# Splitting the gather of the next pair's tokens in a two-layer encoder's mixture of experts

## The chip, the cores and the metric

The kernel runs on one core of one Trainium2 chip. The metric is device time in microseconds (us) from start to end of one execution; the number given for a kernel is the median of its runs. TensorE (PE) does the matmuls, with its weight loads shown apart as PEld; VectorE (DVE) and ScalarE (ACT) read the matmul results out of PSUM; SyncE (SP) issues nearly all transfers from HBM.

## The reference

Two layers over 256 tokens of width 2048, all in float32. Each layer has three mixers (latent attention, dilated attention, an mLSTM), an output projection, and then the mixture of experts, in which alone this change lies:

```python
comb = jnp.sum(jax.nn.one_hot(eid, N_EXPERTS, dtype=f32) * w[..., None], axis=-2)
h = jax.nn.silu(jnp.einsum('bsd,edf->bsef', x, w_gate)) * jnp.einsum('bsd,edf->bsef', x, w_up)
h = h * comb[..., None].astype(h.dtype)
return jnp.einsum('bsef,efd->bsd', h, w_down)
```

There are 16 experts of width 512, and each token is routed to 2 of them. The gate, up and down weights of all 16 experts are 201 MB per layer (16 x 3 x 2048 x 512 x 4 bytes), and all of them are read from HBM in each layer.

## The kernel before

The five engines each have a program written out by hand, with semaphores between them. The experts are taken in 8 pairs per layer (`i` = 0 to 7). An expert has room for 64 tokens, so that a pair fills the 128 rows of the array: the two experts' matmuls stand alternately in TensorE's program, and each takes half of the columns.

For a pair, TensorE's program holds these blocks: the four products `g0`, `u0`, `g1`, `u1` (the first and second half of gate and up), `gather(i + 1)` (the next pair's tokens, picked out of `xtok` by a matrix of ones and zeros, `Gm`), `turn_h(0)` and `turn_h(1)` (transposes of the gated values), `scatter(i - 1)` in two halves, a transpose of the scatter weights, and the down products `dy0` to `dy3`. The gather writes four PSUM banks (`gx0` to `gx3`, banks 4 to 7, which the down products `dy0` to `dy3` use too), 8 matmuls of 128 columns into each. ScalarE copies these banks into `XG` only behind `u1` of the running pair, since the four products read `XG`. VectorE makes `Gm` in `tokens_of_pair`, with four small operations.

The expert weights come in blocks of 2 MB, 12 for each pair (two for each of `g0`, `u0`, `g1`, `u1`, `dn0`, `dn1`), in exactly that order, issued by SyncE. They land in nine slots, used in turn: six of `ring`, and the space of `BIAS`, `XN` and `PR`, which is why TensorE's rows show these names. A load waits until the block that was nine before it in the same slot has had its last reader. In each layer nine loads go out ahead of the experts; the tenth and eleventh then wait for the end of `g0` of pair 0, the next two for `u0`, the next two for `g1`, the next two for `u1`, and so on:

```python
EXPERT = [f"{n}{j}_{i}" for i in range(NE // 2) for n in ("g0", "u0", "g1", "u1", "dn0", "dn1") for j in range(2)]
EXPERT_SLOTS = (IN_BIAS, 5, 0, 1, 2, 3, 4, IN_XN, IN_PR)
```

All matmuls of the products, the gather, the scatter and the down products are recorded under one line (L642, the helper `mm`). They are told apart by their operands and shapes: the gather's read `v_mla` and `PR` (`Gm` lies in `v_mla`, the tokens in `PR`), those of the four products have the shape 128x256 at 64 weights' columns, the down products 128x512. One float32 matmul of the program is two records of the trace. `turn_h` is L986, the transpose of the scatter weights L1026. On VectorE, L1589 multiplies gate and up, and L1565 makes `Gm` and the scatter weights; SyncE's loads are L568.

Of the kernel before, what the change touches and what calls it, by code (L numbers as in the profile page):

```python
# [52 lines left out]
NE = NG * EPG  # L53
# [281 lines left out]
def build(nc, a, consts, onehot, lncount, out):  # L335
    with ExitStack() as ctx:
# [143 lines left out]
        def after(name, l, j=0, i=None, stride=0):  # L480

            s, n = stages[name]
            return s, l * n + (j + 1) + (0 if i is None else i * stride)
# [9 lines left out]
        def bank(name):  # L493
            return ps[:, BANKS.where(name), :]

        def ready(name, l=0):

            return psum_full[BANKS.where(name)], BANKS.before(name, l) + 1

        def freed(name, l=0):  # L500

            return psum_free[BANKS.where(name)], BANKS.before(name, l)

        def copied(name, l=0):

            return psum_free[BANKS.where(name)], BANKS.before(name, l) + 1

        def made(name):
            return psum_full[BANKS.where(name)], 1
# [4 lines left out]
        def slot(name):  # L514
            s = SLOTS.where(name)
            return ring[:, s, :] if s < NSLOT else spare[s]
# [15 lines left out]
        def loaded(name, l):  # L532
            s = SLOTS.where(name)
            return slot_full[s], 16 * (SLOTS.before(name, l) + 1)
# [105 lines left out]
        def _(pe):  # L640
            def mm(o, lhsT, rhs, start=True, stop=True):
                return pe.matmul(o, lhsT, rhs, start=start, stop=stop, skip_group_check=True)  # L642
# [154 lines left out]
            for l in range(DEPTH):  # L797
# [154 lines left out]
                mm(o[:, 2 * NE:3 * NE], ones[:, :], picked[:, 0, 0:NE], True, False)  # L952
                mm(o[:, 2 * NE:3 * NE], ones[:, :], picked[:, 1, 0:NE], False, True).then_inc(*made("rank"))

                def gather(i):

                    pe.wait_ge(*after("gm", l, i))
                    for n in range(4):
                        name = f"gx{n}_{i}"
                        pe.wait_ge(*freed(name, l))  # L960
                        for k in range(4):
                            d = (4 * n + k) * P
                            for t in range(NT):
                                last = mm(bank(name)[:, k * 2 * CAP:(k + 1) * 2 * CAP], xtok[:, t, d:d + P], Gm[:, t, :], t == 0, t == NT - 1)
                        last.then_inc(*made(name))

                def expert(n, i):

                    name = f"{n}_{i}"
                    w = [slot(f"{n}{j}_{i}").rearrange("p (k c) -> p k c", k=KT) for j in range(2)]  # L970
                    for j in range(2):
                        pe.wait_ge(*loaded(f"{n}{j}_{i}", l))
                    pe.wait_ge(*freed(name, l))
                    for k in range(KT):
                        for j in range(2):
                            own_rows = slice(j * CAP, (j + 1) * CAP)
                            last = mm(bank(name)[own_rows, 0:CH], XG[:, k, own_rows], w[j][:, k, :], k == 0, k == KT - 1)
                    last.then_inc(*made(name))

                def turn_h(half, i):  # L980

                    name = f"ht{half}_{i}"
                    pe.wait_ge(*copied(f"u{half}_{i}", l))
                    pe.wait_ge(*freed(name, l))
                    for q in range(2):
                        last = pe.transpose(bank(name)[:, q * 2 * CAP:(q + 1) * 2 * CAP], gated[:, (2 * half + q) * P:(2 * half + q + 1) * P], ident)  # L986
                    last.then_inc(*made(name))

                def scatter(i, ks):

                    for k in ks:
                        name = f"sc{k}_{i}"
                        pe.wait_ge(*freed(name, l))
                        for q in range(2):
                            last = mm(bank(name)[:, q * S:(q + 1) * S], Y[:, (2 * k + q) * P:(2 * k + q + 1) * P], Sw)
                        last.then_inc(*made(name))

                def written(i):
                    pe.wait_ge(*copied(f"sw_{i}", l))
                    for n in range(4):  # L1000
                        pe.wait_ge(*copied(f"dy{n}_{i}", l))
# [4 lines left out]
                for i in range(NE // 2):  # L1006
                    for n in range(4):
                        pe.wait_ge(*copied(f"gx{n}_{i}", l))
                    expert("g0", i)
                    expert("u0", i)  # L1010
                    expert("g1", i)
                    turn_h(0, i)
                    if i + 1 < NE // 2:
                        gather(i + 1)
                    expert("u1", i)
                    if i >= 1:
                        written(i - 1)
                        scatter(i - 1, range(KT // 4))
                    turn_h(1, i)
                    if i >= 1:  # L1020
                        scatter(i - 1, range(KT // 4, KT // 2))

                    pe.wait_ge(*freed(f"sw_{i}", l))
                    pe.wait_ge(*after("gw", l, i))
                    for t in range(NT):
                        last = pe.transpose(bank(f"sw_{i}")[0:2 * CAP, t * P:(t + 1) * P], Gw[:, t, :], ident)  # L1026
                    last.then_inc(*made(f"sw_{i}"))

                    for half in range(2):
                        pe.wait_ge(*copied(f"ht{half}_{i}", l))  # L1030
                    for half in range(2):
                        w = [slot(f"dn{half}{j}_{i}").rearrange("p (k c) -> p k c", k=4) for j in range(2)]
                        for j in range(2):
                            pe.wait_ge(*loaded(f"dn{half}{j}_{i}", l))
                        for q in range(2):
                            name = f"dy{2 * half + q}_{i}"
                            pe.wait_ge(*freed(name, l))
                            for k in range(4):
                                for j in range(2):
                                    own_rows = slice(j * CAP, (j + 1) * CAP)  # L1040
                                    last = mm(bank(name)[own_rows, :], hs[:, k, own_rows], w[j][:, k, q * 512:(q + 1) * 512], k == 0, k == 3)
                            last.then_inc(*made(name))
# [3 lines left out]
                with pe.If(due > 0):  # L1046

                    i = NE // 2 - 1
# [72 lines left out]
        def _(dve):  # L1121
# [121 lines left out]
            for l in range(DEPTH):  # L1243
# [324 lines left out]
                def tokens_of_pair(i):  # L1568
                    for j in range(2):
                        ins = one_hot(Gm[:, :, j * CAP:(j + 1) * CAP], 2 * i + j, seen)  # L1570
                    ins.then_inc(*signal("gm"))
# [10 lines left out]
                for n in (1, 3):  # L1582
                    gathered(f"gx{n}_0", n, l)
                for i in range(NE // 2):
                    for half in range(2):

                        dve.wait_ge(*copied(f"g{half}_{i}", l))
                        dve.wait_ge(*ready(f"u{half}_{i}", l))
                        dve.tensor_tensor(gated[:, half * CH:(half + 1) * CH], sgs[:, half * CH:(half + 1) * CH],  # L1589
                                          bank(f"u{half}_{i}")[0:2 * CAP, 0:CH], ALU.mult).then_inc(*read(f"u{half}_{i}"))  # L1590
                        if half == 0:
                            if i + 1 < NE // 2:
                                tokens_of_pair(i + 1)
                            for j in range(2):
                                ins = one_hot(Gw[:, :, j * CAP:(j + 1) * CAP], 2 * i + j, comb)
                            ins.then_inc(*signal("gw"))
                        elif i >= 1:
                            add_moe(i - 1, range(KT // 4))
                        dve.wait_ge(*ready(f"ht{half}_{i}", l))
                        dve.tensor_copy(hs[:, 2 * half:2 * half + 2, :].rearrange("p k n -> p (k n)"), bank(f"ht{half}_{i}")[:, 0:4 * CAP]).then_inc(*read(f"ht{half}_{i}"))  # L1600
                    if i >= 1:
                        add_moe(i - 1, range(KT // 4, KT // 2))
                    dve.wait_ge(*ready(f"sw_{i}", l))
                    dve.tensor_copy(Sw, bank(f"sw_{i}")[0:2 * CAP, 0:S]).then_inc(*read(f"sw_{i}"))
                    for n in (1, 3):
                        dve.wait_ge(*ready(f"dy{n}_{i}", l))
                        dve.tensor_copy(Y[:, n * 512:(n + 1) * 512], bank(f"dy{n}_{i}")[0:2 * CAP, :]).then_inc(*read(f"dy{n}_{i}"))  # L1607
# [356 lines left out]
```

## Time and profile before

| | |
|---|---|
| median of 3 runs | 1985.12 us (1984.39 to 1989.51) |
| the profiled execution | 1986.55 us, with a span of 1984.9 us |
| TensorE busy (matmuls) | 1929.6 us, 97% of the span |
| TensorE weight loads | 1457.5 us, 73% |
| VectorE, ScalarE, GpSimd busy | 472.4, 317.6 and 5.8 us |
| read from HBM | 534.49 MB, 270 GB/s over the span |
| mean granted TensorE clock | 0.989 of full speed |

The busy time of TensorE counts modelled ends of pipelined matmuls, so a busy share near 100% doesn't say that nothing waits: waits are read from the chain and from the start times. The expert stages of the two layers lie at about 538 to 990 us and 1521 to 1985 us. There the transfers are read for their rate (GB/s in a window), and each load for the time from its issue to its landing.

### The profile page before, as it was taken

What the parts mean: (1) busy time and instruction counts of PE and PEld (TensorE: products, weight loads), DVE (VectorE), ACT (ScalarE), POOL (GpSimd) and SP (SyncE); (2) the same over time, 40 slices, a digit from 0 to 9 for tenths busy, and PEclk for the clock granted to TensorE, in tenths of its full rate; (3) what the DMA queues carried; (4) which work ended last, traced back from release to release, by engine and by line L of the source; (5) the groups of instructions that cost most, each with busy time, mean ns of one, the idle gap of its engine ahead of it and who ended that gap; (6) DMA issues with size and microseconds to landing.
All of it is one profiled execution on the core that took longest, in us unless ns stands there. A gap on an engine that the chain in (4) does not pass through costs nothing.

```text
span 1984.9 us, 26562 instructions
## 1 busy us (share of the span) xinstructions
PE 1929.6 (97%) x11730; PEld 1457.5 (73%) x11730; DVE 472.4 (24%) x1233; ACT 317.6 (16%) x831; POOL 5.8 (0%) x12
## 2 busy tenths in 40 slices
PE   6999999999899999999899999999998999999998
PEld 6788888788766666656597888877887666666665
DVE  2233313122211111221133232222222012110212
ACT  2122122210211110111021221222102111110110
POOL 0000000000000000000000000000000000000000
PEclk9999999999899999999999999999998999999999
DMA  8353333223599999999963433322346999999995
GB/s 330 137 209 127 128 127 127 92 106 149 212 414 427 428 426 427 428 427 427 413 238 146 151 116 137 130 88 88 128 157 255 426 426 427 426 428 426 428 427 242
DMA packets 39831, 538.39 MB, mean 271 GB/s; under 512 B 4665, under 2 KB 4793, under 8 KB 7201
## 3 DMA queue, kind: packets, MB, share of 16 engines
q1 hardware_dynamic: 38160, 531.46, 65.3%
q0 software_dynamic: 1296, 5.13, 0.7%
q8 instruction: 97, 1.59, 0.3%
q14 instruction: 22, 0.17, 0.0%
q10 hardware_dynamic: 256, 0.04, 0.0%
HBM read 534.49 MB, written 2.12 MB: 270 GB/s over the span
## 4 chain that ended last, share of the span: by engine, by line
PE 97%; issue 1%; DVE 1%; DMA 1%; ACT 0%; SPq 0%; DVEq 0%
PE ps L642 94%; PE ps L693 1%; DMA ring<-in_w_lat 1%; PE ps L986 0%; PE ps L709 0%; PE ps L701 0%; PE ps L907 0%; PE ps L1026 0%; ACT PR L1849 0%; PE ps L780 0%; ACT L1862 0%; SPq L562 0%; DVE v_mla L1565 0%; PE ps L820 0%; DVE prob L1607 0%
## 5 line engine op out<-in xcount | busy, mean ns | idle before, releaser
L642 PE MATMUL ps<-ring,scr 128*64 128x256 f32 (+2 forms) x3520 | 562.7, 428 | 7.1 <-issue 7.1
L642 PE MATMUL ps<-ring,XN 128*128 128x256 f32 (+2 forms) x2304 | 484.6, 371 | 17.1 <-DMA ring<-in_w_lat 17.1
L642 PEld LDWEIGHTS ps<-ring,XN 128*128 128x128 f32 x2304 | 424.5, 191 | 66.9 <-issue 19.1
L642 PEld LDWEIGHTS ps<-ring,scr 128*64 128x64 f32 (+1 forms) x3520 | 319.8, 139 | 203.9 <-issue 113.2
L642 PE MATMUL ps<-XN,ring 128*128 128x256 f32 x768 | 170.4, 381 | 0.9 <-DVE prob L1155 0.9
L642 PE MATMUL ps<-BIAS,scr 128*64 128x256 f32 (+1 forms) x608 | 159.3, 420 | 6.9 <-issue 6.9
L642 PEld LDWEIGHTS ps<-XN,ring 128*128 128x128 f32 x768 | 144.7, 190 | 26.6 <-issue 7.7
L642 PE MATMUL ps<-PR,scr 128*64 128x256 f32 (+2 forms) x576 | 158.3, 430 | 0.7 <-DVE scr L1600 0.7
L642 PE MATMUL ps<-PR,ring 128*128 128x256 f32 x640 | 142.9, 383 | 0.0
L642 PE MATMUL ps<-XN,scr 128*64 128x256 f32 (+1 forms) x576 | 141.6, 403 | 0.3 <-issue 0.2
L642 PEld LDWEIGHTS ps<-PR,ring 128*128 128x128 f32 x640 | 121.9, 192 | 19.1 <-issue 2.7
L642 PE MATMUL ps<-v_mla,PR 128*128 128x128 f32 x1024 | 122.7, 283 | 4.1 <-DVE v_mla L1565 4.1
L642 PEld LDWEIGHTS ps<-v_mla,PR 128*128 128x128 f32 x1024 | 121.2, 200 | 4.2 <-issue 4.2
L642 PE MATMUL ps<-PR,prob 128*128 128x256 f32 x512 | 118.7, 386 | 5.0 <-issue 3.8
L1589 DVE TENSOR_TENSOR v_mla<-scr,ps 128x256 f32<-128x256 f32 x32 | 13.5, 421 | 429.8 <-PE ps L642 429.8
L642 PEld LDWEIGHTS ps<-PR,prob 128*128 128x128 f32 x512 | 96.0, 192 | 24.2 <-issue 12.1
L642 PEld LDWEIGHTS ps<-BIAS,scr 128*64 128x64 f32 x608 | 83.6, 139 | 34.2 <-issue 9.9
L642 PEld LDWEIGHTS ps<-PR,scr 128*64 128x64 f32 (+1 forms) x576 | 81.2, 146 | 34.6 <-issue 24.9
L642 PEld LDWEIGHTS ps<-XN,scr 128*64 128x64 f32 x576 | 78.3, 137 | 29.4 <-issue 19.5
L1874 ACT ACTIVATE scr<-ps,par 128x128 f32<-128x128 f32 x240 | 63.8, 412 | 222.7 <-PE ps L642 222.7
L1578 DVE TENSOR_TENSOR X<-X,ps 128x512 f32<-128x512 f32 x128 | 87.9, 687 | 31.9 <-PE ps L642 31.0
L1882 ACT ACTIVATE scr<-ps 128x256 f32<-128x256 f32 x32 | 12.3, 383 | 378.7 <-PE ps L642 378.7
(231 smaller groups left out, 1009.7 us busy)
## 6 DMA issues: line engine op xcount, KB each, us to landing
ring<-in_moe_w_up SPq DMA_DIRECT2D x44, 2048.0 KB, 22.7
ring<-in_moe_w_down SPq DMA_DIRECT2D x44, 2048.0 KB, 26.5
ring<-in_moe_w_gate SPq DMA_DIRECT2D x42, 2048.0 KB, 24.5
ring<-in_w_main SPq DMA_DIRECT2D x36, 2048.0 KB, 8.1
ring<-in_w_out_a SPq DMA_DIRECT2D x10, 2048.0 KB, 8.0
PR<-in_moe_w_down SPq DMA_DIRECT2D x10, 2048.0 KB, 24.2
XN<-in_moe_w_gate SPq DMA_DIRECT2D x10, 2048.0 KB, 28.2
BIAS<-in_moe_w_up SPq DMA_DIRECT2D x10, 2048.0 KB, 23.4
```

Source lines behind the costliest of these rows:

```text
L642: return pe.matmul(o, lhsT, rhs, start=start, stop=stop, skip_group_check=True)
L693: last = pe.transpose(bank(name)[:, (kt * NT + t) * P:(kt * NT + t + 1) * P], prob[:, u % 2, j, t, kt * P:(kt + 1) * P], ident)
L1578: dve.tensor_tensor(x, x, bank(name), ALU.add).then_inc(*read(name))
L1589: dve.tensor_tensor(gated[:, half * CH:(half + 1) * CH], sgs[:, half * CH:(half + 1) * CH], bank(f"u{half}_{i}")[0:2 * CAP, 0:CH], ALU.mul ...
L1874: ins = act.activation(XG[:, 4 * n + k, :], bank(name)[:, k * 2 * CAP:(k + 1) * 2 * CAP], ACT.Copy, scale=pcol(l, R_FFN + 4 * n + k))
L1882: act.activation(sgs[:, half * CH:(half + 1) * CH], bank(f"g{half}_{i}")[0:2 * CAP, 0:CH], ACT.Silu).then_inc(*read(f"g{half}_{i}"))
```

## The change

The gather of the next pair is called in two halves, two of its four PSUM banks each. The first half stands behind `g0`, the second behind `u0`; before, the whole gather stood behind `turn_h(0)`, between `g1` and `u1`. So that `Gm` is there in time, VectorE makes it at the head of the pair, ahead of the multiplication of gate and up, and waits first until the four banks of this pair's own gather are complete (its matmuls are the last readers of the old `Gm`). The number of matmuls, copies and loads stays the same. The last pair of a layer gathers nothing and keeps its order.

```diff
-                def gather(i):
+                def gather(i, ns=range(4)):
 
                     pe.wait_ge(*after("gm", l, i))
-                    for n in range(4):
+                    for n in ns:
...
                     expert("g0", i)
+                    if i + 1 < NE // 2:
+                        gather(i + 1, (0, 1))
                     expert("u0", i)
+                    if i + 1 < NE // 2:
+                        gather(i + 1, (2, 3))
                     expert("g1", i)
                     turn_h(0, i)
-                    if i + 1 < NE // 2:
-                        gather(i + 1)
                     expert("u1", i)
...
                 for i in range(NE // 2):
+                    if i + 1 < NE // 2:
+                        for n in range(4):
+                            dve.wait_ge(*ready(f"gx{n}_{i}", l))
+                        tokens_of_pair(i + 1)
                     for half in range(2):
...
                         if half == 0:
-                            if i + 1 < NE // 2:
-                                tokens_of_pair(i + 1)
                             for j in range(2):
```

On TensorE, in pair 0 of the first layer, the rows behind the last matmul of `g0` read as follows before (`u0` and `g1` are the matmuls on `ring`, the first of the 65 still belongs to `g0`; the row on `K,v_mla` is `turn_h(0)`, the row on `v_mla,PR` the gather, and the rows behind it begin `u1`):

```order
L642 MATMUL ps<-ring,scr 64x256 x65
L986 MATMUL ps<-K,v_mla 128x128 x2
L642 MATMUL ps<-v_mla,PR 128x128 x32
L642 MATMUL ps<-ring,scr 64x256
L642 MATMUL ps<-XN,scr 64x256
```

The same place on TensorE after the change:

```order
L642 MATMUL ps<-ring,scr 64x256
L642 MATMUL ps<-v_mla,PR 128x128 x16
L642 MATMUL ps<-ring,scr 64x256 x32
L642 MATMUL ps<-v_mla,PR 128x128 x16
L642 MATMUL ps<-ring,scr 64x256 x32
L986 MATMUL ps<-K,v_mla 128x128 x2
L642 MATMUL ps<-ring,scr 64x256
L642 MATMUL ps<-XN,scr 64x256
```

`u0` now stands behind 16 gather matmuls and `g1` behind 32, while `u1` follows `turn_h(0)` at once, behind the same number of matmuls as before.

On VectorE, the start of pair 0 before (L1589 is the multiplication of gate and up, L1565 makes `Gm` for the next pair and then the scatter weights, L1600 copies the turned values):

```order
L1589 TENSOR_TENSOR v_mla<-scr,ps 128x256 [waits psum_full1,psum_free0]
L1565 TENSOR_SCALAR v_mla<-PR 128x64 x8
L1600 COPY scr<-ps 128x256 [waits psum_full0]
L1589 TENSOR_TENSOR v_mla<-scr,ps 128x256 [waits psum_full3,psum_free2]
```

And after, where the same lines have the numbers L1595, L1567 and L1604:

```order
L1567 TENSOR_SCALAR v_mla<-PR 128x64 [waits psum_full6,psum_full7,psum_full5,psum_full4]
L1567 TENSOR_SCALAR v_mla<-PR 128x64 x3
L1595 TENSOR_TENSOR v_mla<-scr,ps 128x256 [waits psum_full1,psum_free0]
L1567 TENSOR_SCALAR v_mla<-PR 128x64 x4
L1604 COPY scr<-ps 128x256 [waits psum_full0]
```

Four of the eight small operations moved ahead of the multiplication, behind a wait for the four banks of the gather that has just been used.

## Rows read from the trace of the kernel before

**Rows 1.** The page: mean busy share of the DMA engines in 40 slices

```profile
DMA  8353333223599999999963433322346999999995
```

**Rows 2.** Windows: from:to, length, busy PE, PEld, DVE, ACT, POOL (count), PEclk, DMA share, GB/s

```profile
535.00:546.00 11.00, 9.95 (x93) 8.26 (x94) 0.69 (x1) 2.81 (x6) 0.00 (x0) 1.00 0.01 1
546.50:576.00 29.50, 28.47 (x256) 22.44 (x254) 3.81 (x13) 2.44 (x10) 0.00 (x0) 1.00 1.00 415
...
577.00:700.00 123.00, 123.00 (x892) 80.09 (x889) 21.90 (x47) 14.60 (x47) 0.00 (x0) 1.00 1.00 426
...
830.00:960.00 130.00, 123.86 (x916) 82.10 (x916) 22.94 (x52) 12.78 (x41) 0.00 (x0) 0.99 1.01 428
```

**Rows 3.** The chain in order of time, first layer: start, us, what

```profile
745.56 0.22 PE ps L1026 x2
...
802.28 0.22 PE ps L1026 x2
...
830.20 1.63 issue
...
888.77 1.98 issue
890.75 8.81 PE ps L642 x64
...
949.60 7.13 PE ps L642 x64
...
957.10 2.30 issue
959.40 12.46 PE ps L642 x80
```

**Rows 4.** The chain in order of time, second layer

```profile
1812.94 0.62 issue
...
1870.98 2.65 issue
...
1939.87 2.50 issue
```

**Rows 5.** Time to landing: loads issued at 545.5, 552.4, 559.3, 573.9 and 935.6

```profile
DMA to landing us min/median/max: 8.1/8.1/8.1
...
DMA to landing us min/median/max: 12.0/12.0/12.0
...
DMA to landing us min/median/max: 14.9/14.9/14.9
...
DMA to landing us min/median/max: 10.1/10.1/10.1
...
DMA to landing us min/median/max: 23.7/23.7/23.7
```

**Rows 6.** Timeline of SyncE: start, us, and the loads issued from then on

```profile
545.54 0.33 SPq L568 DMA_DIRECT2D BIAS<-in_moe_w_down  x1
545.91 6.86 SPq L568 DMA_DIRECT2D ring<-in_moe_w_down  x2
552.82 6.86 SPq L568 DMA_DIRECT2D ring<-in_moe_w_gate  x2
559.72 14.54 SPq L568 DMA_DIRECT2D ring<-in_moe_w_up  x2
```

**Rows 7.** Timeline of TensorE in pair 0: the gather of pair 1

```profile
559.52 7.31 PE L642 MATMUL ps<-v_mla,PR 128*128 128x128 f32 x64
```

**Rows 8.** Windows of 1 us, and of the last `g1` and `u1` of the layer (columns as in rows 2)

```profile
1559.00:1560.00 1.00, 1.00 (x6) 0.35 (x4) 0.00 (x0) 1.00 (x6) 0.00 (x0) 1.00 1.07 295
...
949.60:956.50 6.90, 6.90 (x64) 5.38 (x64) 1.21 (x5) 0.00 (x0) 0.00 (x0) 1.00 1.01 425
...
959.40:968.10 8.70, 8.70 (x64) 6.42 (x64) 0.00 (x0) 0.00 (x0) 0.00 (x0) 0.80 1.01 429
```

**Rows 9.** Timeline of VectorE in pair 2: copy of `dy3`, and the small operations

```profile
646.27 0.69 DVE L1607 COPY prob<-ps 128x512 f32<-128x512 f32 x1 [6.17 <-PE ps L642]
...
660.49 1.87 DVE L1565 TENSOR_SCALAR v_mla<-PR 128x64 f32<-128x64 f32 x8
```

## The prediction

> **What bounds the kernel now.** I read the page first: TensorE is 97% busy, and in the two expert stages the DMA engines are at 9 of 10 in every slice, where they are at 2 to 4 in most of the others [rows 1]. So two things may bound these stages, and the page can't say which. The windows say more of the transfers: nothing moves between 535 and 546 us, and from 546.5 us on the rate is 415, then 426, then 428 GB/s to the end of the layer's experts [rows 2]. From 546.5 us the DMA engines never stop, while TensorE still has spare time in the last 130 us (123.9 of 130 us busy).
>
> The chain in order of time says where TensorE waits. In the middle pairs it waits for nothing: the same row of two successive pairs stands 56.72 us apart (745.56, 802.28). Late in the layer three pieces "issue" appear, 1.63, 1.98 and 2.30 us, ahead of `g1` of pairs 5 and 6 and of `u1` of pair 7 [rows 3]. The second layer has the same places, with 0.62, 2.65 and 2.50 us [rows 4]. They are waits for weights. The load issued at 935.6 us lands 23.7 us later, at 959.3 us, and `u1` of pair 7 starts at 959.40 us [rows 3, 5]. Counted in order, that load is 76 places behind the one issued at 573.9 us, which landed 10.1 us later, at 584.0 us [rows 5]. So one load of 2 MB takes (959.3 - 584.0) / 76 = 4.94 us of the stream, and the 12 of a pair take 59.3 us. TensorE needs 56.7 us for a pair. It eats up the lead of the prefetch by 2.5 us a pair, and from pair 5 on it waits.
>
> Hence the last wait, `u1` of pair 7, is the one that sets the end of the layer. Its time is that of its load, which is the time at which the stream began to run without a pause, plus a fixed number of loads. The earlier waits don't add to it: TensorE, had it not waited before, would only wait longer there.
>
> **The change part by part.** *What moves on TensorE.* A gather takes 7.31 us [rows 7], half of it 3.66 us. `u0` ends 3.66 us later than before, `g1` 7.31 us later, `u1` at the same time. In pairs 5 and 6 this puts 7.3 us of work ahead of `g1`, where the waits of 1.63 and 1.98 us stand, so these vanish. Pair 7 has no gather, its order is unchanged, and the load that it waits for comes when the stream delivers it. By the argument above the vanished waits reappear in pair 7. The gain from them is 0.
>
> *What it does to the stream.* Here is the price. In pair 0 the stream is fed by the slots that `g0`, `u0`, `g1` and `u1` let go: two loads at 545.5 us, two at 552.4, two at 559.3, two at 573.9 [rows 6] (a row of two loads gives the start of the first alone). The first, alone on idle engines, lands in 8.1 us; the later ones in 12.0, 14.9 and 10.1 us [rows 5]. What they need beyond 8.1 us is the queue ahead of them: 3.9, 6.8 and 2.0 us. After the change the second pair of loads is issued 3.66 us later and the third 7.31 us later. By this count the queue is just not dry at the second (0.2 us left) and dry by 7.31 - 6.8 = 0.5 us at the third. That is the lower bound, 0.5 us a layer. But the count is generous, since a load that follows another lands later behind its own data than a lone one. The second layer shows it: at 1559 us its stream dips to 295 GB/s for one us, 0.3 us lost [rows 8], at the place where the row of the first layer still counts 2.0 us of queue. So I take 1 us off each queue: 5.8 us of cover against 7.31 us of delay, which is 1.5 us of pause per layer, spread over the two places. The upper bound is that each of the two places pays the whole of what a lone load needs beyond its share of the stream, 8.1 - 4.9 = 3.2 us, 6.4 us a layer. I stay near the lower end since the delay is 1.5 us beyond the cover and no more. The fourth pair of loads still has its 2.0 us of queue, now more, and later pairs add 2.5 us of queue each.
>
> [...]
>
> *The clock.* `g1` of pair 6 takes 8.81 us behind its wait, where the same block in pair 7 takes 7.13 us [rows 3]. The granted clock says why: it is 0.80 on average over `u1` of pair 7 and 1.00 over `g1` of pair 7 [rows 8], so that a part of such a block runs at 1.2 instead of 2.4 GHz. Behind waits of 1.98 us and more the clock fell, 1.68 us lost each time; behind 1.63 us it did not. The loss at `u1` of pair 7 lies on the path. Without any wait before it TensorE would reach `g1` of pair 7 at 949.60 - 0.2 - 1.63 - 1.98 - 1.68 = 944.1 us. Four more changes of shape on TensorE per pair, for which I put 0.1 us each (no row isolates one; up to 0.2 us the waits would absorb), make it 946.9 us. The loads for `g0`, `u0`, `g1`, `u1` of pair 7 end 9.9 us apart: 929.6, 939.5, 949.4, 959.3 us, all 1.5 us later now. `g0` doesn't wait, `u0` waits about 1 us, `g1` then comes at 947.9 and waits until 950.9 us, 3 us. The clock then falls there, `g1` takes 8.8 us, and `u1` comes at about 960 us for a load of 960.8 us. That short wait leaves the clock alone. So the 1.68 us disappears from the path in each layer, hidden in a wait. In case the clock falls at `u1` as before, nothing is gained.
>
> *VectorE.* The four small operations take about 0.93 us (half of 1.87 us for eight) and now stand behind the copy of `dy3`, 0.69 us from 646.27 us [rows 9]. `Gm` is ready some 1.7 us into `g0`, which, like the `g1` of [rows 8], runs 6.9 us: cost 0. If that cover were gone, TensorE's queue would wait at the half gather, and `u0` and its release of slots with it. The added wait for the four banks is satisfied a pair earlier. ScalarE still copies into `XG` behind `u1`, as before.
>
> *Sum.* Per layer 1.5 - 1.7 = -0.2 us, for both -0.4 us. Against the profiled execution this is 1986.55 - 0.4 = 1986.2 us, against the median 1985.12 - 0.4 = 1984.7 us. The two differ by 1.4 us, as the runs of before do among each other (1984.39 to 1989.51), and a measurement here can't tell a change under 0.3%, 6 us, from none.
>
> **The rivals.**
>
> *The waits are won back.* If TensorE's waits were its own, all of 1.63 + 1.98 + 2.30 us in the first layer, 0.62 + 2.65 + 2.50 in the second, and the four half clocks of 1.68 us would go: 18.4 us, 1966.7 us. For it: the change puts work exactly where two of the three waits stand. Against it: the stream has no pause between 546.5 us and the last load [rows 2], and the last wait stands in a pair that isn't changed. It would need a stream faster than 428 GB/s, or loads that a slot now holds back late in the layer. Chance 0.07.
>
> *The stream runs dry at full price.* The places are pair 0 of both layers, where `u0` and `g1` let their slots go late. The price is 3.2 us at each of two places in each layer, 12.8 us, with the lower clock on the path as before: 1997.9 us. It decides as soon as the queue ahead of the late loads is truly empty for the engines when they come, and each restart is paid as for a lone load. For it: the cover left is 0.2 us at one place and negative at the other. Against it: part of what a lone load takes beyond 4.9 us is its landing, which doesn't stop the stream. Chance 0.14. [...]
>
> *It changes nothing that matters* because the gather's halves wait for `Gm` or a bank and so stand where they stood. Rows 9 leave over 5 us of cover, and TensorE is the only engine with a full program, so I give it 0.04, at 1985 us.
>
> **How the numbers follow.** The forecast, a stream shifted by 0.5 to 3 us a layer and a clock that falls at `u1` or not, has 0.75 and gives 1984.7 us. Its own range is 1982.7 (0.5 us a layer, clock gained) to 1991.1 (3 us, clock not gained). The whole range starts 2 us under that for the spread of the runs, 1980.5, and ends at 1991.5 us, between forecast and the second rival. The chances: faster by over 0.3% 0.08, slower 0.15, no difference 0.77.
>
> **What would show it.** Of the profile after: no "issue" piece ahead of `g1` of pairs 5 and 6, but pieces ahead of `u0`, `g1` and `u1` of pair 7; the load behind `u1` of pair 7 landing 0.5 to 3 us later, counted from the start of the stream in pair 0; in pair 0 two dips in GB/s, near 556 and 567 us; the loads released by `u0` and `g1` landing in about 8 to 9 us after issue instead of 12.0 and 14.9; the clock falling behind `g1`, not `u1`, of pair 7. The prediction is wrong if `u1` of pair 7 starts without a wait (first rival), or if each dip is 3 us long (second).

## The result, and the profile after

The changed kernel takes 1988.6 us (median of 17 runs, 1985.0 to 1991.56) against 1984.68 us of before in the same rounds. The ratio is 1.0018, with an interval of 1.0010 to 1.0026: slower by 3.6 us, less than 0.3%, but clear of the measurement. The forecast was 0.4 us less than before. So the sign is wrong, though the time lies inside the range (1980.5 to 1991.5 us). The prediction also said that a measurement can't tell a change under 0.3% from none; with 17 runs of each kernel the interval reaches 0.08% to either side.

The windows over the same stretches as [rows 2] come first, with the same columns:

```profile
535.00:546.00 11.00, 9.96 (x90) 8.12 (x89) 1.58 (x5) 2.81 (x6) 0.00 (x0) 1.00 0.00 1
546.50:576.00 29.50, 28.47 (x254) 20.19 (x254) 2.87 (x9) 2.18 (x9) 0.00 (x0) 1.00 0.95 378
577.00:700.00 123.00, 123.00 (x884) 77.66 (x882) 21.91 (x47) 14.46 (x47) 0.00 (x0) 1.00 1.01 428
830.00:960.00 130.00, 125.29 (x941) 80.41 (x940) 21.64 (x47) 12.42 (x40) 0.00 (x0) 1.00 1.01 427
```

The second row is the change. In the first 29.5 us of the stream the transfers moved 378 GB/s instead of 415 [rows 2]; behind that both kernels run at 426 to 428. The missing (415 - 378) x 29.5 us are 2.6 us at 427 GB/s. (The window starts 1.0 us behind the first issue before the change and 1.4 us behind it here; moved to 1.0 us it reads 380 GB/s, and the loss is 2.4 us.) In the second layer the same stretch, from the stream's start, reads 416 before and 384 after, 2.2 us:

```profile
1529.30:1558.80 29.50, 28.47 (x257) 22.43 (x255) 3.81 (x13) 2.50 (x10) 0.00 (x0) 1.00 0.99 416
```

```profile
1532.50:1562.00 29.50, 28.63 (x255) 20.32 (x253) 2.53 (x9) 1.83 (x7) 0.00 (x0) 1.00 0.97 384
```

SyncE's timeline in pair 0 of the first layer answers to [rows 6]:

```profile
545.11 0.33 SPq L568 DMA_DIRECT2D BIAS<-in_moe_w_down  x1
545.48 10.79 SPq L568 DMA_DIRECT2D ring<-in_moe_w_down  x2
556.32 10.78 SPq L568 DMA_DIRECT2D ring<-in_moe_w_gate  x2
567.14 7.38 SPq L568 DMA_DIRECT2D ring<-in_moe_w_up  x2
```

The times to landing of the loads issued at 545.1, 555.9, 566.8 and 574.2 us answer to [rows 5]:

```profile
DMA to landing us min/median/max: 8.2/8.2/8.2
...
DMA to landing us min/median/max: 10.0/10.0/10.0
...
DMA to landing us min/median/max: 11.3/11.3/11.3
...
DMA to landing us min/median/max: 13.6/13.6/13.6
```

The loads released by `u0` and `g1` go out 3.9 and 7.8 us later, counted from the first one. The fourth lands at 574.2 + 13.6 - 545.1 = 42.7 us behind that first issue, against 573.9 + 10.1 - 545.5 = 38.5 us before. The load of `u1` of pair 7 is issued at 934.3 us and takes 28.4 us: 417.6 us behind the first issue, against 959.3 - 545.5 = 413.8 us. The delay of pair 0 is still there 390 us later.

The loads released by `u0` and `g1` take 10.0 and 11.3 us to land. That is less than the 12.0 and 14.9 us of before, as forecast, but more than the "about 8 to 9 us" of the prediction.

The chain in order of time, first layer of the changed kernel, first the pieces that end with `g1` of pairs 5 and 6 (each holds the down products ahead, `g0`, `u0`, `g1` and the gather), then pair 7:

```profile
805.54 42.44 PE ps L642 x320
...
862.95 42.44 PE ps L642 x320
...
920.37 20.79 PE ps L642 x128
941.15 2.05 issue
943.20 7.13 PE ps L642 x64
950.33 2.67 issue
953.00 7.13 PE ps L642 x64
...
960.49 2.27 issue
962.76 12.31 PE ps L642 x80
```

As forecast, the waits ahead of `g1` of pairs 5 and 6 [rows 3] are gone and stand ahead of `u0`, `g1` and `u1` of pair 7 instead (in the second layer ahead of `g1` and `u1` alone, 2.66 and 2.42 us). But `g1` takes 7.13 us behind its wait of 2.67 us, so the clock did not fall there. It fell at `u1`, as before: the granted clock over its first 8.6 us is 0.82 on average. In the second layer it fell at neither. A pair takes 862.95 - 805.54 = 57.41 us instead of 56.72: the four more changes of shape cost 0.69 us a pair, not the 0.4 us of the prediction, and the waits of pair 7 take this up.

### The profile page after: what moved, and what is told of

It is laid out like the page before. It is cut to its first block, busy times and chain, and to the rows that moved or that the text cites. A ratio compares the mean times of both kernels' runs of the same rounds, so it can differ in the third digit from the quotient of the medians.

```text
span 1988.2 us, 26604 instructions
## 1 busy us (share of the span) xinstructions
PE 1932.9 (97%) x11730; PEld 1442.6 (73%) x11730; DVE 472.6 (24%) x1233; ACT 318.0 (16%) x831; POOL 5.8 (0%) x12
## 4 chain that ended last, share of the span: by engine, by line
PE 97%; issue 1%; DVE 1%; DMA 1%; ACT 0%; SPq 0%; DVEq 0%
PE ps L642 94%; PE ps L693 1%; DMA ring<-in_w_lat 1%; PE ps L986 0%; PE ps L709 0%; PE ps L701 0%; PE ps L907 0%; PE ps L1028 0%; ACT PR L1853 0%; SPq L562 0%; PE ps L780 0%; ACT L1866 0%; DVE v_mla L1567 0%; PE ps L820 0%; DVE prob L1611 0%
## 5 line engine op out<-in xcount | busy, mean ns | idle before, releaser
L642 PEld LDWEIGHTS ps<-ring,scr 128*64 128x64 f32 (+1 forms) x3520 | 307.3, 138 | 204.7 <-issue 108.6
L642 PEld LDWEIGHTS ps<-v_mla,PR 128*128 128x128 f32 x1024 | 122.0, 199 | 14.9 <-issue 14.9
L642 PE MATMUL ps<-v_mla,PR 128*128 128x128 f32 x1024 | 127.6, 285 | 4.0 <-DVE v_mla L1567 4.0
L1595 DVE TENSOR_TENSOR v_mla<-scr,ps 128x256 f32<-128x256 f32 x32 | 13.5, 421 | 372.6 <-PE ps L642 372.6
```

## The experiments

In the expectations, "load for u1 of pair 0" is the load that `u1` of pair 0 lets go, the fourth of the list above. "Starved stream" is the theory that the whole loss comes from the late release of slots in pair 0; the rival puts it in the other pairs.

### The split in pairs 1 to 6 alone

```diff
-                    if i + 1 < NE // 2:
+                    if 1 <= i < NE // 2 - 1:
                         gather(i + 1, (0, 1))
                     expert("u0", i)
-                    if i + 1 < NE // 2:
+                    if 1 <= i < NE // 2 - 1:
                         gather(i + 1, (2, 3))
                     expert("g1", i)
                     turn_h(0, i)
+                    if i == 0:
+                        gather(i + 1)
                     expert("u1", i)
```

> The split is kept in pairs 1 to 6, and pair 0 of each layer has its old order on TensorE (whole gather behind turn_h(0)); VectorE stays as in the change. Starved stream (the whole loss comes from pair 0, where u0 and g1 let their slots go late): the load for u1 of pair 0 that was issued 28 us after the first late-released load lands 38.5 us after that load's issue as before, the loads of u1 of pair 7 413.8 us after it, and the time is that of before or up to 3.4 us less, if the clock no longer falls on u1 of pair 7: ratio 0.998 to 1.000. Rival, the cost lies in the pairs (four more changes of shape a pair, and three waits in pair 7 instead of one): the ratio stays near the 1.002 of the change.

Ratio 0.9999 (0.9991 to 1.0008). The window of the stream's first 29.5 us:

```profile
546.50:576.00 29.50, 28.47 (x254) 22.33 (x252) 2.92 (x9) 3.05 (x12) 0.00 (x0) 1.00 0.98 417
```

417 GB/s, about as before the change. The fourth load lands 38.2 us behind the first issue, that of `u1` of pair 7 413.9 us in the first layer and 413.8 us in the second. The clock fell at `u1` of pair 7 in both layers (12.45 and 12.46 us for `u1` and the 16 matmuls behind it, which take 10.78 us at full clock), so the gain that was held possible there did not come. Six of the seven splits cost nothing, with all their extra changes of shape, and bring nothing.

### The split in pair 0 alone

The diff is the counterpart: the two half gathers under `if i == 0`, the whole gather behind `turn_h(0)` under `if 1 <= i < NE // 2 - 1`.

> The counterpart: only pair 0 of each layer is split, pairs 1 to 6 have the old order. Starved stream: the loss of the change is all there, load for u1 of pair 0 landing 40 to 43 us after the first issue instead of 38.5, last load 415.5 to 417.6 us instead of 413.8; the old waits before g1 of pairs 5 and 6 and the fallen clock at u1 of pair 7 come back, so ratio 1.002 to 1.004, at least the change's. Rival (the pairs): ratio 1.000.

Ratio 1.0020 (1.0012 to 1.0029), as much as the whole change. The same window:

```profile
546.50:576.00 29.50, 28.47 (x253) 19.91 (x253) 2.91 (x9) 2.52 (x10) 0.00 (x0) 1.00 0.96 384
```

(At the distance of before from the first issue, from 545.77 us on, it is 380.) The fourth load lands at 41.6 and 41.3 us in the two layers, the load of `u1` of pair 7 at 416.5 and 416.3 us. One split out of seven carries the loss.

### VectorE's part alone

TensorE has the order of before in all pairs; VectorE keeps `tokens_of_pair` at the head of the pair.

> VectorE's part alone: Gm is made at the head of the pair, TensorE keeps the whole gather behind turn_h(0) in all pairs. Both theories: 1.000, within 0.05%. A third, that VectorE's earlier small operations delay the multiplication and with it turn_h, would show here as 1.001 or more and a wait of TensorE ahead of turn_h(0).

Ratio 0.9996 (0.9987 to 1.0006). The earlier operations cost nothing that can be measured.

### A larger dose: the whole gather behind g0 in pair 0

```diff
                     expert("g0", i)
-                    if i + 1 < NE // 2:
-                        gather(i + 1, (0, 1))
+                    if i == 0:
+                        gather(i + 1)
                     expert("u0", i)
-                    if i + 1 < NE // 2:
-                        gather(i + 1, (2, 3))
                     expert("g1", i)
                     turn_h(0, i)
+                    if 1 <= i < NE // 2 - 1:
+                        gather(i + 1)
```

> A larger dose, in pair 0 alone: the whole gather directly behind g0, so that u0 and g1 both let their slots go 7.3 us late; pairs 1 to 6 in the old order. Starved stream: the two loads released by u0 are issued at 14 us after the first pair of loads, whose data take 9.9 us, so the engines stand still for 3.5 us and more plus a restart: one large pause instead of two small ones, load for u1 of pair 0 at 42.5 to 44 us, ratio 1.003 to 1.005. If a pause cost nothing beyond the time in which the queue is empty, 42.0 us. Rival (the pairs): 1.000.

Ratio 1.0029 (1.0018 to 1.0041). Two windows of this kernel, the stream's first 29.5 us and the pause in it:

```profile
546.50:576.00 29.50, 28.47 (x252) 19.90 (x252) 2.92 (x9) 3.15 (x13) 0.00 (x0) 1.00 0.86 357
...
556.50:562.00 5.50, 5.50 (x54) 3.67 (x52) 1.32 (x5) 0.00 (x0) 0.00 (x0) 1.00 0.38 107
```

Here the pause is plain. The stretch as a whole is short of 58 GB/s, or 4.0 us, but in this run the first load is issued 1.1 us earlier (at 544.5 us), and the window leaves out part of the stream's slow start: from 545.48 to 574.98 us it reads 348 GB/s, which is 4.6 us lost. The fourth load lands at 43.5 and 42.6 us, inside the expected 42.5 to 44 us, and on average 1.0 us behind the 42.0 us that would hold if a pause cost no more than its empty time. The loads of `u1` of pair 7 land at 418.4 and 418.3 us, 4.6 and 4.3 us late. Of these 8.9 us the time shows 5.8. One part of the difference is the clock (the table in the section on the prediction); the rest stays open.

### A smaller dose: g1 alone late, and within the cover

```diff
                     expert("g0", i)
-                    if i + 1 < NE // 2:
-                        gather(i + 1, (0, 1))
                     expert("u0", i)
-                    if i + 1 < NE // 2:
-                        gather(i + 1, (2, 3))
+                    if i == 0:
+                        gather(i + 1, (0, 1))
                     expert("g1", i)
                     turn_h(0, i)
+                    if i == 0:
+                        gather(i + 1, (2, 3))
+                    elif i + 1 < NE // 2:
+                        gather(i + 1)
```

> A smaller dose, in pair 0 alone: its first half gather stands behind u0, its second behind turn_h(0), so that u0 lets its slots go at the old time and g1 3.7 us late, where the queue ahead has 6.8 us by the count of the prediction; pairs 1 to 6 in the old order. Starved stream with a threshold at the cover: no pause, load for u1 of pair 0 at 38.5 us, ratio 1.000. Rival, each late release costs in proportion whatever the cover: about 40 us, and ratio 1.001.

Ratio 1.0004 (0.9995 to 1.0014). The window is moved by 0.8 us, since the stream begins later in this run (the first load is issued at 545.9 us); over the window of the others it reads 415 GB/s, as before:

```profile
547.30:576.80 29.50, 28.47 (x254) 21.23 (x251) 2.92 (x9) 2.58 (x10) 0.00 (x0) 1.00 0.99 419
```

The fourth load lands at 38.2 us in both layers. So the loss is no matter of lateness in itself: 3.9 us late at `g1` is free, where the queue ahead is long enough. The rival of a price in proportion falls by the landing (it had about 40 us); the ratio alone would leave room for its 1.001.

### The changed kernel, twice more

> The changed kernel, unedited, profiled once more, for two numbers that one profile can't give: how long the pauses of pair 0 are, and how often the clock falls at u1 of pair 7. Theory (the price of the two restarts varies, 1.9 and 4.2 us in the two layers so far): load for u1 of pair 0 between 40 and 43.5 us in both layers, never at 38.5. For the clock: if the length of the wait alone decided, every wait of more than 2 us in pair 7 would be followed by a block of 8.4 us or more; the first profile had three that were not and one that was, so I expect both cases again.

> The same once more, with the same expectation: load for u1 of pair 0 at 40 to 43.5 us behind the first issue in both layers, and waits of over 2 us in pair 7 with and without a fallen clock behind them.

One run each, 1984.47 and 1987.21 us. The fourth load lands at 41.5 and 41.3 us in the first, 41.5 and 41.8 us in the second; with 42.7 and 40.5 us of the first profile that is 41.6 us on average, 3.1 us behind the 38.5 of before. The load of `u1` of pair 7 lands at 415.5, 416.3, 416.0 and 416.7 us, with the first profile's 417.6 and 415.6 at 416.3 us on average, 2.4 us behind 413.9. Part of the loss is made up on the way, and what does so stays open.

The chain of the first of these runs, second layer, pair 7:

```profile
1921.81 0.79 issue
1922.60 7.13 PE ps L642 x64
1929.73 2.67 issue
1932.40 8.81 PE ps L642 x64
...
1941.58 0.60 issue
1942.18 10.78 PE ps L642 x80
```

This is the case that the prediction had worked out, with a granted clock of 0.80 over `g1` and 1.00 over `u1`: the clock falls behind `g1`, whose block takes 8.81 us, the wait for `u1` shrinks to 0.60 us, and `u1` runs at full clock. Of six layers of the changed kernel, three went so, two had no fallen clock in pair 7 at all, and one had it at `u1`. (Of the waits of over 2 us in the first profile, four had no fallen clock behind them and not three, as the expectation counts: 2.05 and 2.67 us in the first layer, 2.66 and 2.42 us in the second.)

### Filling the wait that is left

By the account so far the waits of pair 7 are the only ones at the end of a layer that cost anything, and behind them stands work that needs no further load. So the scatter of pair 6 can stand ahead of `u1`.

```diff
+                    if i == NE // 2 - 1:
+                        written(i - 1)
+                        scatter(i - 1, range(KT // 2))
                     expert("u1", i)
-                    if i >= 1:
+                    if 1 <= i < NE // 2 - 1:
                         written(i - 1)
                         scatter(i - 1, range(KT // 4))
                     turn_h(1, i)
-                    if i >= 1:
+                    if 1 <= i < NE // 2 - 1:
                         scatter(i - 1, range(KT // 4, KT // 2))
...
                     for half in range(2):
 
+                        if half == 1 and i == NE // 2 - 1:
+                            add_moe(i - 1, range(KT // 2))
                         dve.wait_ge(*copied(f"g{half}_{i}", l))
```

VectorE's two old `add_moe(i - 1, ...)` get the condition `1 <= i < NE // 2 - 1` as well. This is the kernel before with that move:

> The kernel before, with one move in pair 7 alone: the whole scatter of pair 6 stands ahead of u1 instead of behind it, in the time in which TensorE waits for the load of u1, and VectorE adds it ahead of its second multiplication. If the end hangs on the last load of u1 plus what is behind it: the wait of 2.3 us goes, u1 starts 4.6 us later, 6.9 us less stand behind it, so 2.3 us gained a layer, and 1.7 us more where the clock had fallen there: ratio 0.996 to 0.998. In the first layer the load of dn1, which lands at 982.3 us for a block that starts at 982.6 us, takes most of it back: 0.997 to 0.999. Rival (the end of the layer hangs on TensorE's own work): 1.000.

Ratio 0.9974 (0.9966 to 0.9983), 5.2 us gained. Its chain in pair 7 of the second layer:

```profile
1929.40 0.68 issue
1930.09 7.13 PE ps L642 x64
...
1937.58 13.99 PE ps L642 x96
```

The 2.50 us ahead of `u1` [rows 4] are gone: the 13.99 us are the scatter and `u1` without a pause, and without a fallen clock.

The same with the split in pairs 1 to 6, and with GpSimd's reload of `BIAS` waiting for `dy3` of pair 7:

> The split in pairs 1 to 6, with the whole scatter of pair 6 ahead of u1 of pair 7, and GpSimd's reload of BIAS moved from the end of u1 to the end of dy3 of pair 7, so that it doesn't share the stream with the last expert loads. Stream theory: 1.9 and 2.3 us of waits stand in pair 7, of which this fills the second: 2.2 us a layer and the clock at u1, ratio 0.996 to 0.998, and unlike in the run before it, the first layer keeps its share. Rival: 1.000.

Ratio 0.9970 (0.9960 to 0.9980), 1978.57 us, the fastest kernel of the study. Without the split, but with the later reload:

> The kernel before with the scatter of pair 6 ahead of u1 of pair 7, and GpSimd's reload of BIAS behind dy3: fill_from_1 without the split in pairs 1 to 6. It tells what the split is worth where it does no harm. If the waits ahead of g1 of pairs 5 and 6 don't count (stream theory), the ratio is that of fill_from_1, 0.997, within 0.1%. If the split there is worth its 3.6 us of waits and a clock of 1.7 us a layer, it is 0.999 or more.

Ratio 0.9973 (0.9964 to 0.9983): the two can't be told apart, nor from the first fill. The split in pairs 1 to 6 is worth nothing measurable here either. Last, the scatter spread over two waits, with its PSUM banks planned anew (`sc0` to `sc3` of pair 6 in banks 2 and 3 ahead of `g1`, the others in banks 1 and 0 behind `turn_h(0)`):

> As the run before it, but the scatter of pair 6 is spread in pair 7: its first half ahead of g1, its second behind turn_h(0), ahead of u1, in other PSUM banks. Both waits of pair 7 (1.9 and 2.3 us) are filled: 4.2 us a layer, and 1.7 us where the clock fell at u1: ratio 0.994 to 0.9965. Rival: 1.000, or as fill_from_1 if the waits of pair 7 only move.

Ratio 0.9973 (0.9964 to 0.9983), a smaller gain than the 0.994 to 0.9965 that I expected. The chain of its last pair in the first layer says where the next wait is:

```profile
971.50 7.09 PE ps L649 x32
978.59 1.16 issue
979.74 7.10 PE ps L649 x32
```

TensorE now waits between `dy1` and `dy2`, for the last load of the layer. That load, the very end of the stream, is what binds once `u1` comes early enough: it lands at 979.6 us, and `dy2` starts at 979.74 us. An order on TensorE that leaves the stream as it is can't get round it.

## Why the prediction was wrong

**The bound was right.** The expert stage ends with its stream of loads, and TensorE's waits in pairs 5 and 6 were worth nothing. The split without pair 0 took them away and the time stayed (0.9999), with the last `u1` load at 413.9 and 413.8 us. The rival that wins them back would have given 18 us.

**The place and the sign of the price were right.** Pair 0 carries all of the loss, in two dips where `u0` and `g1` let their slots go late, and a release within its cover is free.

**The step that failed is the sum of the two terms, "1.5 - 1.7 = -0.2 us" per layer.** Both were mis-sized, in the same direction.

*The pause, put at 1.5 us a layer (7.31 us of delay less 5.8 us of cover).* It measures 2.4 to 2.6 and 2.2 us by bytes in the first profile, and 2.4 us at the last `u1` load over six layers. The 1.5 us counted only the time in which the queue is empty. It left out that a stream which starts again runs slowly at first. Before the change there is one such start a layer, and these windows of the kernel before show it:

```profile
546.50:549.00 2.50, 2.50 (x27) 1.97 (x25) 0.00 (x0) 0.00 (x0) 0.00 (x0) 1.00 1.00 282
549.00:551.00 2.00, 2.00 (x22) 1.60 (x20) 0.00 (x0) 0.00 (x0) 0.00 (x0) 1.00 0.99 426
```

282 GB/s in the first 2.5 us, 426 behind: 2.5 x (1 - 282/427) = 0.85 us lost. The changed kernel's two dips in the first layer look alike, here first their deepest parts and then each dip as a whole:

```profile
556.50:559.50 3.00, 3.00 (x29) 2.98 (x27) 0.84 (x4) 0.00 (x0) 0.00 (x0) 1.00 0.93 295
567.50:569.50 2.00, 2.00 (x22) 1.34 (x20) 0.06 (x1) 0.00 (x0) 0.00 (x0) 1.00 0.96 295
...
556.00:560.00 4.00, 4.00 (x36) 3.81 (x38) 1.31 (x5) 0.00 (x0) 0.00 (x0) 1.00 0.89 303
567.00:571.00 4.00, 4.00 (x39) 2.69 (x40) 0.42 (x1) 0.16 (x1) 0.00 (x0) 1.00 0.91 320
```

In the two whole dips 4 x (1 - 303/427) = 1.2 us and 4 x (1 - 320/427) = 1.0 us are lost, 2.2 of the 2.4 us. By the shares of 0.89 and 0.91 the engines stood idle for 0.8 us of this, and the other 1.4 us went at a low rate. So the empty time was shorter than the 1.5 us of the prediction, and the slow restarts, which it left out, were the larger part. (The shares are coarse over 4 us, so the division is an estimate.) The whole gather behind `g0` says the same from another side, with its 1.0 us beyond the empty time. The row on the start was there before the prediction; I had read the window from 546.5 to 576 us as a whole, 415 GB/s, and a DMA share of 1.00 looked like a full stream. The delay itself was also a little more than the 7.31 us of the gather: 7.8 us, for the changes of shape, which I had counted on TensorE but not on the release of the slots.

*The clock, put at 1.7 us gained in each layer.* This table sets layers against the same layer of the kernel before. The end of a stage is taken at the start of VectorE's copy of `dy3` of pair 7 (989.69 us in the first layer before, 992.89 us after), and all is counted from the first issue in pair 0 of the layer:

| kernel, layer | last `u1` load later by | clock at `u1` | stage ends later by |
|---|---|---|---|
| changed, 1 | 3.8 us | fell | 3.6 us |
| changed, 2 | 1.6 us | stayed | 0.0 us |
| first repeat, 1 and 2 | 1.7 and 2.3 us | stayed | 0.8 and 0.6 us |
| second repeat, 1 and 2 | 2.2 and 2.7 us | stayed | 1.3 and 1.0 us |
| split in pair 0 alone, 1 and 2 | 2.7 and 2.3 us | fell | 2.7 and 2.3 us |
| whole gather behind `g0`, 1 | 4.6 us | fell | 4.6 us |
| whole gather behind `g0`, 2 | 4.3 us | stayed | 2.6 us |

Where the clock fell at `u1`, as it did in both layers of before, the stage ends later by the delay of the stream; where it stayed, by about 1.7 us less. In the first layers of the two repeats it is 0.9 us less, since TensorE waits another 0.5 us for the last load of the layer. So both terms of the sum exist, and the clock's 1.7 us has the right size where it comes. What was wrong is how often it comes. The case of the prediction, a fall at `g1` in its place, was met in three of six layers, and with the two layers in which the clock didn't fall at all `u1` was spared five times out of six. But the old order doesn't pay it each time either. Of the ten profiled layers of the five kernels that run pairs 5 to 7 in the old order, without a fill, the clock fell at `u1` in eight, so the gain is an estimated (8/10 - 1/6) x 1.7 = 1.1 us a layer, not 1.7. It isn't the split of the late pairs that brings it: with the split in pairs 1 to 6 alone the clock fell at `u1` in both layers. There the wait ahead of `g1` was 1.94 and 1.87 us, in the six layers of the changed kernel it was 2.65 to 2.67 us. The longer wait, itself a result of the pause in pair 0, may be what spares `u1`, but that is not shown: in the second layer of the whole gather behind `g0`, `u1` was spared too, with a wait of 1.93 us ahead of `g1`.

With both terms as measured the sum is 2 x (2.4 - 1.1) = 2.6 us, and by the stage ends of the six layers it is 2.4 us, both inside the interval of 2.0 to 5.2 us (0.0010 and 0.0026 of 1985 us). Neither term put right alone gives a sum inside the interval: with 2.4 and 1.7 us it is 1.4 us, with 1.5 and 1.1 us it is 0.8 us. Where the last microsecond up to the measured 3.6 lies stays open. The spans of the two first profiles differ by 1988.2 - 1984.9 = 3.3 us. The intervals are too wide to see the clock in the times: the split in pair 0 alone, where it fell twice, has 1.0020 against the 1.0018 of the whole change.

That the time lies inside the range is owed to the range's slow end, which allowed 3 us of pause and no gain from the clock, and not to the sum. (The lower end is 0.2 us off: 1982.7 less 2 us is 1980.7.)

**VectorE** cost nothing, as said. The second rival, with 3.2 us at each of the two places, was too dear: its two places make 6.4 us a layer, and even the whole gather behind `g0`, with its plain pause, cost the stream 4.5 us. By the missing bytes the runs show 1.2 to 1.3 us for each of the two places in the first layer.

## What to carry to other kernels

Where a ring of slots is refilled as blocks are used up, the order of the blocks on the engine is also the order in which transfers are issued. Before moving work ahead of a block, compare the delay with the queue ahead of the load that the block releases, at the one place where that queue is shortest: here the first pair, while the waits that the eye goes to stand at the other end of the layer. In a stage that ends with its stream, take waits away only behind the last loads: moving work that needs no load into the last wait gained 0.3%, where splitting six gathers gained nothing.

## What was not expected of the hardware

A stream of 2 MB loads that starts on idle engines runs at 282 GB/s for 2.5 us before it reaches 426, while the DMA share reads 1.00 and 0.99. In the second layer the same 282 GB/s stand beside a share of 0.73 (1529.5 to 1532 us), so over so short a window the share is no measure of the rate. And the length of TensorE's wait doesn't settle whether its clock falls: in pair 7 of the first layer of the changed kernel it stayed at full speed behind 2.05 and 2.67 us and fell behind 2.27 us; in another run of the same kernel it fell behind 2.67 us in one layer and stayed behind 2.67 and 2.30 us in the other. What else decides it stays open.
